# Coefficients placed three products sooner, a Gelu of one column ahead of each unit's Gelu, and the queries and keys in memory of their own

## The chip, the cores and the metric

The kernel runs on one core of one Trainium2 chip. The metric is the device time of one execution, in microseconds (us), with the median over several executions.

## What is computed

One inference step of two layers over 288 tokens: 256 tokens of a prompt and 8 sequences of 4 tokens each. Each layer has a token mixer (a gated convolution in the first layer, RWKV-7 in the second) and behind it a PEER channel mixer, which is the part that the change touches. Cut to that part:

```python
q = (hc @ wq).reshape(-1, PEER_HEADS, D_QUERY)
s1 = jnp.einsum('chd,hkd->chk', q[..., :half], k1)
s2 = jnp.einsum('chd,hkd->chk', q[..., half:], k2)
v1, i1 = lax.top_k(s1, PEER_TOPK)
v2, i2 = lax.top_k(s2, PEER_TOPK)
...
sc, ci = lax.top_k(cand, PEER_TOPK)      # the best 16 of 16 x 16 sums
eidx = e1 * N_KEYS + e2                  # 16 experts of 16384 per token and head
gate = jax.nn.softmax(sc, axis=-1)
z = jax.nn.gelu(jnp.einsum('cd,chkd->chk', hc, u_tab[eidx]), approximate=False)
coef = gate * z
return jnp.einsum('chk,chkd->cd', coef, v_tab[eidx])
```

Every token reads, for each of 8 heads, 16 rows of the table U and 16 rows of the table V, each row 1024 numbers in float32 (4 KB).

## The kernel before

**Units.** The 288 tokens times 8 heads make 2304 pairs, cut into 18 units of 128 pairs, one pair to a partition; the loop over them is `for lu in range(UNITS)` on every engine, and `u = u0 + lu` counts over both layers. A unit has 16 experts per pair, k = 0 to 15. For each k GpSimd issues one indirect transfer from U and one from V (`gather`, L1775), 128 rows of 4 KB each: 0.524 MB. So a unit is 32 transfers, 16.78 MB. U rows go to a ring of 8 slots, V rows to another ring of 8 slots, both in the buffer `ARENA`.

**Order on GpSimd.** Its queue is written by hand: in the steady part V(u, 0), U(u+1, 0), V(u, 1), U(u+1, 1), and so on (`experts` under `block.gpsimd`). It works in order. V(u, k) waits until the slot of product k-8 is free (`v_free`), U(u+1, k) until VectorE has used the slot of k-8 (`s_z`).

**VectorE** (`unit` in `experts` under `block.vector`) multiplies each landed U row with the token's row of h and sums it: `z_of(u + 1, k)`, L1380. Between these 16 products it does the small work of three units in order: it picks the experts of unit u+3 (`choose`, one piece behind each product from k = 3 on, the last piece, GX at L1331, behind product 15), spreads the indices of unit u+1 (`spread_indices`, L1359), turns them into V indices (`v_indices`, L1363), multiplies the Gelu of unit u with its gates (`spread_coefs`, L1368) and places the coefficients of unit u in the matrix ST (`place_coefs`, L1372).

**ScalarE** takes, for each unit, the Exp of GX for the softmax of unit u+3 (`gate_exp`, L1023) and the Gelu of the unit's 16 sums (L1058). Both need tables of their own, loaded by ACT_TABLE_LOAD.

**TensorE** regroups indices (`regroup_indices`, L580) and coefficients (`regroup_coefs`, L590) from pair to token order with four small products each, and then multiplies ST with the landed V rows: per unit four batches q = 0 to 3 of four k each, eight products a batch on four column groups at a time (L675). A batch frees its four V slots at its end, all at once:

```python
for q in range(TOPK // BATCH):
    for i in range(2):
        for j in range(BATCH):
            ...
            m = pe.matmul(ps[QUAD * j:QUAD * (j + 1), ACC_BANK + i, :], ST[:, k, :], ...)
    m.then_inc(v_free, BATCH)
```

**Start of a layer's experts.** The queries `Q4` and the keys `KT` lie in V slots 0 to 3, so the transfers V(0, 4) and later wait until the scores of all units are made, and the queue of GpSimd holds U(1, 0 to 11) ahead of them.

Of the kernel before, what the change touches and what calls it, by code (L numbers as in the profile page):

```python
# [8 lines left out]
ACT = mybir.ActivationFunctionType  # L9
# [139 lines left out]
def build(nc, a, out):  # L149
    with ExitStack() as ctx:  # L150
# [22 lines left out]

        N_RV, N_ROWS, N_SEL = 2 * RING * D, 3 * D, 2880
        ARENA = sb("ARENA", [N_RV + 2 * N_ROWS + N_SEL])
        RV = ARENA[:, 0:N_RV]
        OACC = ARENA[:, N_RV + N_ROWS:N_RV + 2 * N_ROWS].rearrange("p (a d) -> p a d", a=3)
        CURU = sb("CURU", [2, TOPK], U32)
# [33 lines left out]
        CS = carve(2 * DC * TOK + DC * UHW + DC * TOK, [DC * NS_TOK])  # L212
        Q4 = carve(RING * D, [4, TOK])
        KT = carve(RING * D + 1536, [2, HEADS, NKEYS])

        QP = carve(N_RV + N_ROWS, [16, P])
        HROW = ps[:, ROW_BANK:ROW_BANK + 2, :].rearrange("p b n -> p (b n)")


        sel0 = N_RV + 2 * N_ROWS  # L220
        SCUR = carve(sel0, [2, 2, NKEYS])
# [61 lines left out]
        OMKA = sb("OMKA", [DC])  # L283
        gst = sb("gst", [3, WHEADS])

        s_sh, s_shr = sem("shift_columns_ready"), sem("shift_rows_out")
# [41 lines left out]
        s_z = sem("z_done")  # L328
        s_gelu = sem("gelu_ready")
        s_im, s_ixp = sem("indices_spread"), sem("indices_regrouped")  # L330
        s_cm, s_cfp = sem("coefs_spread"), sem("coefs_regrouped")
# [154 lines left out]
        def _(pe):  # L486
# [85 lines left out]
            def regroup_indices(u):  # L572

                pe.wait_ge(s_im, u + 1)
                if u > 0:
                    pe.wait_ge(s_vidx, u)
                if u > 1:
                    pe.wait_ge(s_st, u - 1)
                for kk in range(4):
                    m = pe.matmul(ps[QUAD * kk:QUAD * (kk + 1), REGROUP_BANK, 0:TOPK], TURN[:, kk], IM.rearrange("p (q k) j -> p k q j", k=4)[:, kk],  # L580
                                  start=True, stop=True)
                m.then_inc(s_ixp, 1)

            def regroup_coefs(u):
                pe.wait_ge(s_cm, u + 1)
                if u > 0:
                    pe.wait_ge(s_st, u)
                pe.wait_ge(s_vidx, u + 2 if (u + 1) % UNITS else u + 1)
                for kk in range(4):
                    m = pe.matmul(ps[QUAD * kk:QUAD * (kk + 1), REGROUP_BANK, TOPK:2 * TOPK], TURN[:, kk], CM.rearrange("p (q k) j -> p k q j", k=4)[:, kk],  # L590
                                  start=True, stop=True)
                m.then_inc(s_cfp, 1)

            def experts(layer):
# [64 lines left out]
                for lu in range(UNITS):  # L659
                    u = u0 + lu  # L660
                    if lu in (7, 15):
                        rows_of_h((lu + 1) // 8)
                    if lu + 1 < UNITS:
                        regroup_indices(u + 1)
                    regroup_coefs(u)
# [3 lines left out]
# [3 lines that stand above are left out]
                                k = BATCH * q + j  # L672
                                if i == 0:
# [3 lines left out]
                                              stop=(lu in TILE_ENDS and q == 3), skip_group_check=True)  # L677
                        m.then_inc(v_free, BATCH)

                pe.wait_ge(acc_free, 2 * 3 * (layer + 1))  # L680
# [239 lines left out]
        def _(act):  # L920
# [85 lines left out]
            def experts(layer):  # L1006
# [48 lines left out]
                for lu in range(UNITS):  # L1055
                    u = u0 + lu
                    act.wait_ge(s_z, u * 16 + 16)
                    act.activation(GL[:, lu % 2, :], ZB[:, lu % 2, :], ACT.Gelu).then_inc(s_gelu, 1)  # L1058
# [107 lines left out]
        def _(v):  # L1166
# [183 lines left out]
            def experts(layer):  # L1350
# [56 lines left out]
                def unit(lu):  # L1407
# [7 lines left out]
                    else:  # L1415
                        chosen = choose(u + 3, layer) if lu + 3 < UNITS else iter(())
                    for k in range(TOPK):
                        if k == 2:
                            spread_coefs(u)
                            if 0 < lu and lu + 2 < UNITS:  # L1420
                                choose_ends(u + 2)
                        if k == 1:
                            spread_indices(u + 1)
                        if k == 3:
                            v_indices(u + 1)
                        if k == 5:
                            place_coefs(u)
                        z_of(u + 1, k)
# [290 lines left out]
        def _(pool):  # L1719
# [58 lines left out]
            def experts(layer):  # L1778
# [12 lines left out]
                def get_v(lu, k):  # L1791
                    u = u0 + lu
                    if k == 0:
                        pool.wait_ge(s_vidx, u + 1)
                    if lu == 0 and k == BATCH:

                        pool.wait_ge(bank_ready, GROUP[f"sc{layer}"] + 9)

                    pool.wait_ge(v_free, u * 16 + (k + 1))
                    gather(RVV, v_slot(k), v_tab, CURV[:, u % 2, k:k + 1], v_land)  # L1800

                for k in range(TOPK):
                    get_u(0, k)
                for k in range(BATCH):
                    get_v(0, k)
                for k in range(12):
                    get_u(1, k)
                for k in range(BATCH, TOPK):
                    get_v(0, k)
                    if k < 2 * BATCH:  # L1810
                        get_u(1, k + 8)
                for lu in range(1, UNITS):
# [73 lines left out]
```

## Time and profile before

| | |
|---|---|
| median of 3 runs | 2634.44 us (2632.85 to 2634.78) |
| the profiled execution | 2637.65 us, its span 2635.6 us |
| TensorE | 1690.9 us busy, 64% |
| VectorE | 1401.7 us busy, 53% |
| GpSimd | 1097.6 us busy, 42% |
| ScalarE | 307.3 us busy, 12% |
| queue of the indirect transfers | 604.05 MB, 59.5% of 16 DMA engines over the span |
| experts of the first layer | from 254 us to about 1100 us |
| RWKV layer's mixer | between about 1110 us and 1740 us, hardly any transfers |
| experts of the second layer | from 1783 us to about 2615 us |

Busy shares over the whole span mix stages with different limits. The columns to read here are those of a stretch: the share and the GB/s of the DMA engines, and beside an instruction the idle time of its engine before it and what ended that.

### The profile page before, as it was taken

Reading aid. Unit: us, or ns where it says so; the run is one execution under the profiler, and the core shown is the slowest. Engines: PE = TensorE matmul, PEld = TensorE weight load, DVE = VectorE, ACT = ScalarE, POOL = GpSimd, SP = SyncE. Lnnn points to the kernel's source line nnn. Section 1 sums busy time; section 2 is a strip of 40 time slices with the busy share of each in tenths; the row PEclk is TensorE's granted clock in tenths of the full one; section 3 lists DMA queues with packets and bytes.
Section 4 is the critical chain, followed back from the end, with each engine's and each line's share of the span. In section 5 each row is a group of like instructions: output and inputs, shape, how many; then the busy total and the mean of one; then the engine's idle time right before and its main releaser. Section 6 shows DMA issues by size and latency. Waiting matters only on the chain.

```text
span 2635.6 us, 23280 instructions
## 1 busy us (share of the span) xinstructions
PE 1690.9 (64%) x8416; PEld 877.0 (33%) x8416; DVE 1401.7 (53%) x3441; ACT 307.3 (12%) x589; POOL 1097.6 (42%) x1215
## 2 busy tenths in 40 slices
PE   6998754545354544699589897788545454444546
PEld 3776500000000010276389896466001010000102
DVE  1042766666666664322862634725766666666643
ACT  2211100000100000113221211012000001000000
POOL 2001566766666665300000000004666666666663
PEclk7999876667766676899789997699667666676668
DMA  8653899999999999724100002426999999999996
GB/s 358 282 205 123 337 357 371 381 372 374 383 359 385 366 387 384 264 109 159 57 1 1 1 1 106 160 79 241 366 390 357 387 366 386 362 389 365 384 365 249
DMA packets 177377, 722.65 MB, mean 274 GB/s; under 512 B 19824, under 2 KB 20336, under 8 KB 170480
## 3 DMA queue, kind: packets, MB, share of 16 engines
q0 software_dynamic: 165888, 604.05, 59.5%
q1 hardware_dynamic: 9216, 108.88, 10.5%
q10 hardware_dynamic: 2160, 8.24, 0.8%
q8 instruction: 67, 1.10, 0.2%
q14 instruction: 46, 0.38, 0.0%
HBM read 715.09 MB, written 6.01 MB: 274 GB/s over the span
## 4 chain that ended last, share of the span: by engine, by line
PE 36%; POOL 21%; DMA 18%; DVE 13%; issue 10%; ACT 1%; DVEq 0%; SPq 0%; POOLq 0%; ACTq 0%
POOL ARENA L1775 21%; PE ps L554 15%; DMA ARENA<-in_peer_u,CURU 14%; PE ps L675 6%; PE ps L790 5%; DVE ARENA L1380 3%; DMA ARENA<-in_peer_v,CURV 3%; DMA W<-in_w_ada 1%; PE ps L513 1%; PE ps L523 1%; DVE ST L1372 1%; PE ps L539 1%; PE ps L645 1%; DVE ARENA L1516 1%; PE ps L884 1%
## 5 line engine op out<-in xcount | busy, mean ns | idle before, releaser
L675 PE MATMUL ps<-ARENA,ST 128*32 128x512 f32 x2304 | 749.0, 881 | 563.7 <-DMA ARENA<-in_peer_v,CURV 364.7
L1775 POOL DMA_INDIRECT ARENA<-in_peer_u,CURU x576 | 540.7, 939 | 1141.3 <-DVE GX L1331 924.8
L1380 DVE SCALAR_TENSOR_TENSOR ARENA<-ARENA,ps 128x1024 f32<-128x1024 f32 x576 | 700.7, 1220 | 544.9 <-DMA ARENA<-in_peer_u,CURU 539.4
L1775 POOL DMA_INDIRECT ARENA<-in_peer_v,CURV x576 | 541.1, 939 | 364.0 <-PE ps L675 205.4
L675 PEld LDWEIGHTS ps<-ARENA,ST 128*32 128x32 f32 x2304 | 127.0, 140 | 1139.5 <-DMA ARENA<-in_peer_v,CURV 742.2
L554 PE MATMUL ps<-H,W 128*128 128x288 f32 x1024 | 261.0, 418 | 2.8 <-DVEq L1704 2.8
L554 PEld LDWEIGHTS ps<-H,W 128*128 128x128 f32 x1024 | 199.9, 196 | 58.9 <-DVEq L1704 3.0
L1023 ACT ACTIVATE GX<-GX 128x16 f32<-128x16 f32 x36 | 7.8, 216 | 1237.2 <-DVE GX L1331 1236.9
L790 PE MATMUL ps<-W 128*128 128x128 f32 (+1 forms) x1088 | 132.2, 285 | 20.6 <-DVEq L1176 20.4
L790 PEld LDWEIGHTS ps<-W 128*128 128x128 f32 (+1 forms) x1088 | 128.7, 199 | 24.1 <-DVEq L1176 23.1
L554 PE MATMUL ps<-ARENA,W 128*128 128x288 f32 x512 | 127.5, 413 | 0.0
L590 PE MATMUL ps<-ARENA,CONS 128*32 128x16 f32 x288 | 11.3, 220 | 163.7 <-DVE CURV L1363 163.7
L554 PEld LDWEIGHTS ps<-ARENA,W 128*128 128x128 f32 x512 | 99.0, 194 | 27.7
L1634 DVE TENSOR_TENSOR W<-W,ps 128x512 f32<-128x512 f32 (+1 forms) x76 | 50.6, 666 | 52.0 <-PE ps L790 51.1
L523 PE MATMUL ps<-W,CT 128*32 128x512 f32 x384 | 53.0, 686 | 31.5 <-DVEq L1176 13.1
L1226 DVE SCALAR_TENSOR_TENSOR X<-ps,ADA,X 128x256 f32<-128x256 f32 x32 | 15.5, 484 | 105.3 <-PE ps L554 52.2
L942 ACT ACTIVATE W<-ps 128x512 f32<-128x512 f32 (+2 forms) x81 | 46.5, 574 | 168.1 <-PE ps L790 147.4
L1194 DVE SCALAR_TENSOR_TENSOR GA<-ADA,PAR 128x72 f32<-128x72 f32 x4 | 0.9, 233 | 122.4 <-ACTq L1001 87.9
L1459 DVE SCALAR_TENSOR_TENSOR ARENA<-ARENA,PAR,H 128x288 f32<-128x288 f32 x48 | 21.8, 512 | 81.5 <-PE ps L554 80.5
L590 PEld LDWEIGHTS ps<-ARENA,CONS 128*32 128x32 f32 x288 | 8.4, 139 | 169.0 <-issue 166.1
L942 ACT ACTIVATE ARENA<-ps 128x288 f32<-128x288 f32 (+3 forms) x74 | 37.2, 516 | 182.4 <-PE ps L554 85.8
L580 PE MATMUL ps<-ARENA,CONS 128*32 128x16 f32 x288 | 9.8, 203 | 70.9 <-DVE ARENA L1359 70.9
(268 smaller groups left out, 1731.7 us busy)
## 6 DMA issues: line engine op xcount, KB each, us to landing
W<-in_w_ada SPq DMA_DIRECT2D x24, 2048.0 KB, 11.0
W<-in_peer_wq SPq DMA_DIRECT2D x8, 2048.0 KB, 8.1
W<-in_conv_w_in SPq DMA_DIRECT2D x6, 2048.0 KB, 14.1
ARENA<-in_peer_u,CURU POOLq DMA_INDIRECT x576, 6.9
ARENA<-in_peer_v,CURV POOLq DMA_INDIRECT x576, 6.9
W<-in_conv_w_out SPq DMA_DIRECT2D x2, 2048.0 KB, 9.9
W<-in_rwkv_wr SPq DMA_DIRECT2D x2, 2048.0 KB, 13.3
W<-in_rwkv_wk SPq DMA_DIRECT2D x2, 2048.0 KB, 9.5
```

What stands on the lines that cost most here:

```text
L513: m = pe.matmul(o[:, m4 * NCOND:(m4 + 1) * NCOND], ADR[j % 2][:, m4 * P:(m4 + 1) * P], sel[:, 0:NCOND], start=True, stop=True)
L523: m = pe.matmul(o[QUAD * g:QUAD * (g + 1), :], CT[:, k, 0:QUAD], W[:, t % WRING, k, :], start=(k < 4), stop=(k >= 4))
L539: m = pe.matmul(o[:, 0:TOK], ones[:], SQ[:, c, :], start=(c == 0), stop=(c == DC - 1))
L554: m = pe.matmul(o[:, 0:TOK], W[:, t % WRING, k, (m0 % 4) * P:(m0 % 4 + 1) * P], rhs[:, k, :], start=(k == 0), stop=(k == DC - 1))
L645: m = pe.matmul(o[:, j * P:(j + 1) * P], query_of(layer, 2 * h + half)[:, tile * P:(tile + 1) * P], KT[:, half, h, :], start=True, stop=True)
L675: m = pe.matmul(ps[QUAD * j:QUAD * (j + 1), ACC_BANK + i, :], ST[:, k, :], RVV[:, v_slot(k), i * 512:(i + 1) * 512], start=(lu % 8 == 0 an ...
L790: m = pe.matmul(o[0:n, j * n:(j + 1) * n], l[:, j, :], r[:, j, :], start=True, stop=True)
L884: pe.matmul(o, ART[:, c % 2, q].rearrange("p r t -> p (r t)"), SS[:, c % 2, q, :], start=(q == 0), stop=False, skip_group_check=True)
L942: act.activation(dst, src(o), func, **kw).then_inc(free, 1)
L1380: v.scalar_tensor_tensor(RU[:, k % RING, :], RU[:, k % RING, :], 1.0, HROW, ALU.mult, ALU.mult, accum_out=ZB[:, u % 2, k:k + 1]).then_inc( ...
L1634: V.do(v.tensor_tensor(dst, dst, o, ALU.add))
L1775: pool.indirect_dma_start(ring[:, slot, :], None, tab, bass.IndirectOffsetOnAxis(ap=idx, axis=0)).then_inc(landed[slot], 16)
```

## The change

It has four parts. On VectorE `spread_coefs(u)` moves from ahead of product 2 to ahead of product 1, `place_coefs(u)` from ahead of product 5 to ahead of product 2, `spread_indices(u + 1)` from product 1 to product 4 and `v_indices(u + 1)` from product 3 to product 8. On TensorE `regroup_indices(u + 1)` moves from ahead of unit u's coefficients to behind its second batch. On ScalarE a Gelu of one column stands ahead of the wait for the unit's sums. In `ARENA` the queries and keys get columns of their own, so GpSimd's queue at a layer's start issues V(0, 0 to 7), then U(1, 0 to 7), then V(0, k) and U(1, k) in turn.

```diff
-        N_RV, N_ROWS, N_SEL = 2 * RING * D, 3 * D, 2880
-        ARENA = sb("ARENA", [N_RV + 2 * N_ROWS + N_SEL])
+        N_RV, N_QK, N_ROWS, N_SEL = 2 * RING * D, 4 * TOK + 2048, 3 * D, 2752
+        ARENA = sb("ARENA", [N_RV + N_QK + N_ROWS + N_SEL])
...
-        Q4 = carve(RING * D, [4, TOK])
-        KT = carve(RING * D + 1536, [2, HEADS, NKEYS])
+        Q4 = carve(N_RV, [4, TOK])
+        KT = carve(N_RV + 4 * TOK, [2, HEADS, NKEYS])
...
                 if u > 0:
                     pe.wait_ge(s_vidx, u)
-                if u > 1:
-                    pe.wait_ge(s_st, u - 1)
+                    pe.wait_ge(s_st, u)
...
-                pe.wait_ge(s_vidx, u + 2 if (u + 1) % UNITS else u + 1)
+                pe.wait_ge(s_vidx, u + 1)
...
-                    if lu + 1 < UNITS:
-                        regroup_indices(u + 1)
                     regroup_coefs(u)
...
                         m.then_inc(v_free, BATCH)
+                        if q == 1 and lu + 1 < UNITS:
+                            regroup_indices(u + 1)
...
+                    if u > 0:
+                        act.wait_ge(s_warm, u)
+                    act.activation(warm[:], ident[:, 0:1], ACT.Gelu).then_inc(s_warm, 1)
                     act.wait_ge(s_z, u * 16 + 16)
...
                     for k in range(TOPK):
+                        if k == 1:
+                            spread_coefs(u)
                         if k == 2:
-                            spread_coefs(u)
+                            place_coefs(u)
                             if 0 < lu and lu + 2 < UNITS:
                                 choose_ends(u + 2)
-                        if k == 1:
+                        if k == 4:
                             spread_indices(u + 1)
-                        if k == 3:
+                        if k == 8:
                             v_indices(u + 1)
-                        if k == 5:
-                            place_coefs(u)
                         z_of(u + 1, k)
...
-                    if lu == 0 and k == BATCH:
-
-                        pool.wait_ge(bank_ready, GROUP[f"sc{layer}"] + 9)
-
...
-                for k in range(BATCH):
+                for k in range(RING):
                     get_v(0, k)
-                for k in range(12):
+                for k in range(RING):
                     get_u(1, k)
-                for k in range(BATCH, TOPK):
+                for k in range(RING, TOPK):
                     get_v(0, k)
-                    if k < 2 * BATCH:
-                        get_u(1, k + 8)
+                    get_u(1, k)
```

VectorE in unit 1 of the first layer, before, from the last small pieces behind product 15 on (L1380 is a product, L1359 `spread_indices`, L1368 `spread_coefs`, L1344 `choose_ends`, L1363 `v_indices`, L1372 `place_coefs`):

```order
L1380 SCALAR_TENSOR_TENSOR ARENA,ZB<-ARENA,ps 128x1024
L1359 TENSOR_TENSOR ARENA<-ARENA,CONS 128x64
L1380 SCALAR_TENSOR_TENSOR ARENA,ZB<-ARENA,ps 128x1024
L1368 TENSOR_TENSOR ARENA<-GL,ARENA 128x64
L1344 SCALAR_TENSOR_TENSOR ARENA<-GX,gsm,CONS 128x64
L1380 SCALAR_TENSOR_TENSOR ARENA,ZB<-ARENA,ps 128x1024
L1363 TENSOR_SCALAR CURV<-ps 128x16
L1380 SCALAR_TENSOR_TENSOR ARENA,ZB<-ARENA,ps 128x1024
...
L1380 SCALAR_TENSOR_TENSOR ARENA,ZB<-ARENA,ps 128x1024
L1290 MAX_INDEX ARENA<-ARENA,W 128x8
L1291 MATCH_REPLACE ARENA<-ARENA,W 128x128
L1372 TENSOR_TENSOR ST<-ps,CONS 128x512
```

The same place with the change (lines are four higher: L1384 is a product, L1372 `spread_coefs`, L1376 `place_coefs`, L1348 `choose_ends`, L1363 `spread_indices`):

```order
L1384 SCALAR_TENSOR_TENSOR ARENA,ZB<-ARENA,ps 128x1024
L1372 TENSOR_TENSOR ARENA<-GL,ARENA 128x64
L1384 SCALAR_TENSOR_TENSOR ARENA,ZB<-ARENA,ps 128x1024
L1376 TENSOR_TENSOR ST<-ps,CONS 128x512
L1348 SCALAR_TENSOR_TENSOR ARENA<-GX,gsm,CONS 128x64
L1384 SCALAR_TENSOR_TENSOR ARENA,ZB<-ARENA,ps 128x1024 x2
L1291 MAX ARENA<-W 128x8
L1292 MAX ARENA<-W 128x8
L1363 TENSOR_TENSOR ARENA<-ARENA,CONS 128x64
```

The placing of ST stood behind five products and two pieces of `choose` and now stands behind two products; the two steps for the next unit's indices moved behind it.

TensorE in the first two units, before (L580 is `regroup_indices`, L590 `regroup_coefs`, L675 the products with V):

```order
L655 MATMUL ps<-ARENA 128x128 x16
L580 MATMUL ps<-ARENA,CONS 32x16 x4
L590 MATMUL ps<-ARENA,CONS 32x16 x4
L675 MATMUL ps<-ARENA,ST 32x512 x32
L580 MATMUL ps<-ARENA,CONS 32x16 x4
```

The same place with the change (L581, L591 and L674 are the same three):

```order
L656 MATMUL ps<-ARENA 128x128 x16
L591 MATMUL ps<-ARENA,CONS 32x16 x4
L674 MATMUL ps<-ARENA,ST 32x512 x16
L581 MATMUL ps<-ARENA,CONS 32x16 x4
L674 MATMUL ps<-ARENA,ST 32x512 x16
```

The regrouping of the next unit's indices left the place ahead of the coefficients and splits the unit's 32 products in two halves.

GpSimd at the start of the first layer's experts, before:

```order
L1775 DMA ARENA<-in_peer_u,CURU 128x1024 x16
L1775 DMA ARENA<-in_peer_v,CURV 128x1024 x4
L1775 DMA ARENA<-in_peer_u,CURU 128x1024 x12
L1775 DMA ARENA<-in_peer_v,CURV 128x1024
L1775 DMA ARENA<-in_peer_u,CURU 128x1024
```

The same place with the change:

```order
L1779 DMA ARENA<-in_peer_u,CURU 128x1024 x16
L1779 DMA ARENA<-in_peer_v,CURV 128x1024 x8
L1779 DMA ARENA<-in_peer_u,CURU 128x1024 x8
L1779 DMA ARENA<-in_peer_v,CURV 128x1024
L1779 DMA ARENA<-in_peer_u,CURU 128x1024
```

Four V transfers moved ahead of unit 1's U transfers, and four U transfers moved behind the first V transfer that has to wait for TensorE.

## Rows read from the trace of the kernel before

**Rows 1.** Busy time by stretch: engines, TensorE clock, DMA share, GB/s.

```profile
core 0: us, PE busy (x) PEld busy (x) DVE busy (x) ACT busy (x) POOL busy (x), PEclk, DMA share, GB/s
...
950.35:1000.93 50.58, 21.38 (x148) 5.62 (x142) 24.58 (x61) 1.72 (x3) 29.98 (x32) 0.74 0.98 384
367.05:950.35 583.30, 281.18 (x1051) 52.55 (x1048) 370.93 (x963) 39.93 (x54) 390.76 (x416) 0.67 0.97 374
1891.64:2517.92 626.28, 301.02 (x1195) 58.02 (x1192) 398.88 (x1027) 41.65 (x57) 420.64 (x449) 0.68 0.97 376
1000.93:1046.20 45.27, 22.74 (x83) 4.06 (x82) 22.61 (x39) 1.30 (x3) 29.98 (x32) 0.68 1.02 405
...
1010.00:1045.00 35.00, 17.00 (x62) 3.16 (x65) 17.79 (x32) 1.30 (x3) 23.05 (x25) 0.60 1.03 410
```

**Rows 2.** GpSimd in order of time, unit 9 of the first layer, around its V(u, 8).

```profile
719.21 0.94 POOL L1775 DMA_INDIRECT ARENA<-in_peer_u,CURU  x1 [0.30 <-issue]
...
725.39 0.94 POOL L1775 DMA_INDIRECT ARENA<-in_peer_v,CURV  x1 [5.25 <-PE ps L675]
```

**Rows 3.** GpSimd's waits from 367 to 950 us: total, times, longest.

```profile
POOL ARENA L1775 <- issue: 116.8, 383, 0.3
POOL ARENA L1775 <- PE ps L675: 71.2, 20, 5.7
```

**Rows 4.** The stretch behind that wait, columns as in rows 1.

```profile
725.00:735.00 10.00, 5.73 (x24) 0.96 (x17) 4.98 (x14) 0.00 (x0) 7.48 (x8) 0.84 0.81 270
```

**Rows 5.** The same unit in order of time, ahead of that wait.

```profile
706.24 1.22 DVE L1380 SCALAR_TENSOR_TENSOR ARENA<-ARENA,ps 128x1024 f32<-128x1024 f32 x1 [0.45 <-DMA ARENA<-in_peer_u,CURU]
...
707.78 0.22 ACT L1023 ACTIVATE GX<-GX 128x16 f32<-128x16 f32 x1 [40.81 <-DVE GX L1331]
708.01 1.28 ACT L1058 ACT_TABLE_LOAD   x1
...
708.80 1.22 DVE L1380 SCALAR_TENSOR_TENSOR ARENA<-ARENA,ps 128x1024 f32<-128x1024 f32 x1 [0.40 <-DMA ARENA<-in_peer_u,CURU]
...
709.31 0.22 ACT L1058 ACTIVATE GL<-ZB 128x16 f32<-128x16 f32 x1
...
712.50 0.22 DVE L1368 TENSOR_TENSOR ARENA<-GL,ARENA 128x64 f32<-128x64 f32 x1
...
720.71 0.68 DVE L1372 TENSOR_TENSOR ST<-ps,CONS 128x512 f32<-128x512 f32 x1
...
721.45 6.86 PE L675 MATMUL ps<-ARENA,ST 128*32 128x512 f32 x32 [5.76 <-DVE ST L1372]
```

**Rows 6.** Transfers issued from 1010 to 1045 us: count, median us to landing.

```profile
ARENA<-in_peer_v,CURV POOLq DMA_INDIRECT x12, 8.1
```

**Rows 7.** Two batches' last products, once the fourth V row has landed.

```profile
345.42 1.90 PE L675 MATMUL ps<-ARENA,ST 128*32 128x512 f32 x10 [0.43 <-DMA ARENA<-in_peer_v,CURV]
...
391.13 3.62 PE L675 MATMUL ps<-ARENA,ST 128*32 128x512 f32 x10 [1.10 <-DMA ARENA<-in_peer_v,CURV]
```

**Rows 8.** SyncE's queue from 975 to 1100 us.

```profile
982.99 0.80 SPq L444 DMA_DIRECT2D W<-in_rwkv_wr  x2
```

**Rows 9.** Start of the first layer's experts and the first steady waits, in order of time.

```profile
278.97 1.00 POOL L1775 DMA_INDIRECT ARENA<-in_peer_v,CURV  x1 [0.30 <-issue]
291.12 0.94 POOL L1775 DMA_INDIRECT ARENA<-in_peer_u,CURU  x1 [11.14 <-DVE ARENA L1380]
...
309.36 0.23 DVE L1368 TENSOR_TENSOR ARENA<-GL,ARENA 128x64 f32<-128x64 f32 x1 [6.99 <-ACT GL L1058]
...
313.48 0.94 POOL L1775 DMA_INDIRECT ARENA<-in_peer_v,CURV  x1 [0.30 <-issue]
...
367.05 0.94 POOL L1775 DMA_INDIRECT ARENA<-in_peer_v,CURV  x1 [5.04 <-PE ps L675]
...
1845.13 0.94 POOL L1775 DMA_INDIRECT ARENA<-in_peer_v,CURV  x1 [0.31 <-issue]
...
1891.64 0.93 POOL L1775 DMA_INDIRECT ARENA<-in_peer_v,CURV  x1 [3.91 <-PE ps L675]
```

More of the change, by code:

```diff
@@ L171, in build @@
         W = sb("W", [WRING, DC, 512])
-        N_RV, N_ROWS, N_SEL = 2 * RING * D, 3 * D, 2880
-        ARENA = sb("ARENA", [N_RV + 2 * N_ROWS + N_SEL])
+        N_RV, N_QK, N_ROWS, N_SEL = 2 * RING * D, 4 * TOK + 2048, 3 * D, 2752
+        ARENA = sb("ARENA", [N_RV + N_QK + N_ROWS + N_SEL])
         RV = ARENA[:, 0:N_RV]
-        OACC = ARENA[:, N_RV + N_ROWS:N_RV + 2 * N_ROWS].rearrange("p (a d) -> p a d", a=3)
+        OACC = ARENA[:, N_RV + N_QK:N_RV + N_QK + N_ROWS].rearrange("p (a d) -> p a d", a=3)
         CURU = sb("CURU", [2, TOPK], U32)
@@ L212, in build @@
         CS = carve(2 * DC * TOK + DC * UHW + DC * TOK, [DC * NS_TOK])
-        Q4 = carve(RING * D, [4, TOK])
-        KT = carve(RING * D + 1536, [2, HEADS, NKEYS])
-        QP = carve(N_RV + N_ROWS, [16, P])
+        Q4 = carve(N_RV, [4, TOK])
+        KT = carve(N_RV + 4 * TOK, [2, HEADS, NKEYS])
+        QP = carve(N_RV + N_QK, [16, P])
         HROW = ps[:, ROW_BANK:ROW_BANK + 2, :].rearrange("p b n -> p (b n)")
-        sel0 = N_RV + 2 * N_ROWS
+        sel0 = N_RV + N_QK + N_ROWS
         SCUR = carve(sel0, [2, 2, NKEYS])
@@ L284, in build @@
         gst = sb("gst", [3, WHEADS])
+        warm = sb("warm", [1])
         s_sh, s_shr = sem("shift_columns_ready"), sem("shift_rows_out")
@@ L329, in build @@
         s_gelu = sem("gelu_ready")
+        s_warm = sem("gelu_table_loaded")
         s_im, s_ixp = sem("indices_spread"), sem("indices_regrouped")
```

## The prediction

> **What bounds the kernel now.** I read the busy time by stretch first. The two expert stages fill some 1600 us of the span, and in their steady parts no engine is full: from 367 to 950 us GpSimd is busy 390.8 of 583.3 us, VectorE 370.9, TensorE 281.2 [rows 1]. The DMA engines are: share 0.97 at 374 GB/s. These 583.3 us are 13 units (from V(u, 8) of unit 1 to that of unit 14), 44.87 us each; in the second layer 626.28 us are 14 units, 44.73 us each [rows 1].
>
> Is 374 GB/s the ceiling? No: from 1010 to 1045 us, with nothing held back, the same transfers run at 410 GB/s for 35 us [rows 1]. A unit is 16.78 MB (32 transfers of 0.524 MB), at 410 GB/s 40.9 us, or 1.28 us a transfer. So about 3.9 us of each unit are lost, and the order of time shows where. GpSimd issues U(u+1, 7) at 719.21 and V(u, 8) only at 725.39, idle for 5.25 us, released by TensorE's product with V [rows 2]. The waits give it 71.2 us in 20 times over the 13 units, nearly all in one long wait a unit; the usual gap is 116.8 / 383 = 0.30 us, so an issue takes 0.94 + 0.30 = 1.24 us [rows 2, 3]. Behind the wait the DMA engines starve: 270 GB/s for 10 us [rows 4], (410 - 270) x 10 = 1.4 MB or 3.4 us at 410, most of the 3.9.
>
> What does V(u, 8) wait for? Its slot is freed by batch q = 0 of unit u, which waits for ST, placed at 720.71; TensorE starts at 721.45 [rows 5] though its first rows have landed long ago: V(u, 3) is nine issues ahead of 719.21, at 708.0, and lands 7 to 8 us later. So the placing ends last, and it stands where it does only because VectorE works in order: the coefficients' Gelu was made at 709.31 [rows 5].
>
> **The placing, three products sooner.** Product 0 starts at 708.80 and takes 1.22 us; today `spread_coefs` starts behind product 1, at 712.50 [rows 5]. With the change it comes behind product 0, at about 710.1. The regrouping on TensorE has the whole of product 1 to end in (nothing is ahead of it any more but unit u-1's last batch, whose last V row was issued 2.5 us before V(u, 0)). The placing starts behind product 1, about 712.6, and takes 0.68 us [rows 5]: ST at 713.3 instead of 721.4, 8.1 us sooner. Now the rows end last: V(u, 3) is issued at 708.0. With 8.1 us to landing, what the saturated stretch shows [rows 6], it lands at 716.1. From the landing of a batch's fourth row to its end it takes 3.62 us or 1.90 us [rows 7], by TensorE's clock (0.60 to 0.74 is granted on the mean in these stretches [rows 1], between the levels of 1.2 and 2.4 GHz). So the slots come free at 719.7 or 718.0, and GpSimd wants them at 719.21 + 1.24 = 720.45. The wait is gone, with 0.7 us to spare at the slow clock.
>
> **What then sets the pace.** GpSimd can issue a unit in 32 x 1.24 = 39.8 us, the transfers need 41.0. So the DMA engines fall behind by 1.2 us a unit, landing times grow, and at about 8.8 us GpSimd begins to wait for V slots again, in pieces. Does that cost? With 8.8 us to landing at 1.28 us a transfer about seven transfers are under way; today 8.1 us goes with a full 410 GB/s [rows 1, 6]. A harder case is in the trace too: from 950.35 to 1000.93 two weight tiles (4.19 MB) are loaded beside the gathers [rows 8], GpSimd stands still, and the stretch still moves 384 GB/s with a share of 0.98 [rows 1]; a wait with a full queue costs nothing. I take 41.0 us a unit. Bounds: 39.8 (GpSimd's issue, if the DMA engines could follow) and 44.8 (nothing won).
>
> **Sum.** 13 units of 44.87 to 41.0: -50.3. 14 units of 44.73 to 41.0: -52.2. The unit with the weight tiles has 16.78 + 4.19 = 20.97 MB, 51.2 us at 410, and takes 50.58 today: +0.6. The units behind it in the first layer (45.27 us [rows 1]) and at the same place in the second: -4.3 and -3.7. The last unit of a layer starts from a deeper queue: +1 each, an estimate from 8.8 against 8.1 us, at two landings: +2.
>
> **Start of a layer.** Today V(0, 4 to 7) wait behind U(1, 11) in the queue. With the change they are issued from 280 us on, inside the 11.14 us in which GpSimd waits [rows 9] and the DMA engines run dry. The price: V(0, 8) now stands ahead of U(1, 8 to 11) and waits for batch 0. VectorE gets the Gelu at 309.36 [rows 9], the extra activation adds 0.2; product 1 and the placing add 1.9 (311.5), the batch 3.6: V(0, 8) at 315.2. From there 32 issues lead to V(1, 8), 39.8 us: 355.0, if U(2, 0), due at 337.6, finds its indices. It should: its selection goes two pieces a product from product 6 on and is complete behind product 12, near 334.5. The rest of unit 3's selection (some 6 us behind product 15, near 341) delays unit 1's Gelu to 349 and its batch 0 to about 355.5. So V(1, 8) comes at about 356 instead of 367.05 [rows 9]: -11, of which I take -10. In the second layer V(0, 4) is at 1845.13 against 313.48 in the first, an offset of 1531.65, so V(1, 8) comes at 1887.3 instead of 1891.64 [rows 9]: -4.3. Bounds for both together: -5 (if the held U transfers cost what the V transfers win) and -17.
>
> Sum: -50.3 - 52.2 + 0.6 - 8.0 + 2 - 14.3 = -122.2. The profiled execution takes 2637.65 us, so 2515.4; it lies 3.2 us above the median of 2634.44, so I expect **2512**.
>
> **The Gelu of one column** wins nothing, and I put it at 0. The table load stands at 708.01 because the Exp ahead of it, which needs another table, waits for GX, made behind product 15 (706.24 + 1.22); Exp, load and Gelu follow without a gap [rows 5]. The wait for the unit's sums is over by then, so a load "ahead" of it starts at the same moment, and the Gelu comes 0.22 us later, at 709.53 to 709.75, still before `spread_coefs` wants it at 710.1. If that cover is gone, VectorE waits some tenths, inside the 0.7 us above. In the first unit ScalarE is held by the scores' copies, likewise.
> The trace's load is 1.28 us, and from Exp to Gelu pass 1.53 us [rows 5]. The Trainium skill (ScalarE: Activation LUTs, "What ACT_TABLE_LOAD costs") counts a drain of 1.38 us to each switch, 2.66 us in all. By it the Gelu would come at 711.1 and VectorE would stand still for 1 us behind product 0; the trace shows no such drain, and even then nothing is added to the sum, for product 1 and the placing would still end ahead of V(u, 3)'s landing.
>
> **The indices, later.** `spread_indices` and `v_indices` move behind products 3 and 7. The new V indices are wanted at V(u+1, 0), eight pairs of issues (20 us) after V(u, 8), and product 7 ends some 8 us after V(u, 8): about 12 us of slack stay. Cost 0.
>
> **Rivals.**
> 1. *Part of the wait stays (0.12).* For it: 0.7 us to spare is thin at 1.2 GHz, and a batch frees four slots only at its end. Against it: the waits come with a full queue. If landing is uneven, so that single DMA engines idle, a unit takes 42.5 us: 29 units x 1.5 = 44 more, 2556.
> 2. *The DMA engines follow GpSimd (0.05).* 39.8 us a unit, 1.2 x 29 = 35 less: 2477. Against it: 410 GB/s never moves over 35 us while landing takes 8.1 us.
> 3. *The transfers are at their ceiling already (0.03).* Then the hole is made good elsewhere and only the start gains or nothing: 2620 to 2634. For it: the share is 0.97 today. Against it: the share counts a waiting engine as busy (0.81 at 270 GB/s [rows 4]), and 410 stands beside 374. The Trainium skill (DMA: Bandwidth & Descriptors, "Where 436 GB/s comes from") says the HBM side binds at about 358 GB/s per core for transfers from HBM; by that a unit would need 46.9 us and no order could help. This trace does not agree: 374 on the mean, 410 over 35 us.
> 4. *Slower (0.04): VectorE stalls at `v_indices`.* It now waits, ahead of product 8, for TensorE to end batch 1 of the unit before and regroup. V(u, 7) is issued 1.24 us ahead of U(u+1, 7), so the batch ends up to 3.62 us and the regrouping some 0.5 us after its landing, and VectorE comes to the place 1.28 + 1.22 us and a piece of `choose` (0.8) after it, 3.3: a wait of up to 0.8 us. Behind it stand product 8 and all later ones, and for them wait U slots. The ring of 8 gives 8 x 2.56 = 20.5 us for a landing (8.8), a product (1.2) and the wait: only above 10 us a unit does it hold GpSimd, and only above 14 does it take more than the 3.9 won. At 20 us it would be +6 us in each of 29 units, near 2800. Nothing in the trace makes TensorE so late, unless the two wait in a ring that I don't see.
>
> **How the numbers follow.** The forecast has 0.76; its own range is 2495 to 2535 (41.0 us a unit within 0.5, start within its bounds). With rivals 1 and 2 it makes faster 0.93. A change below 0.2%, 5 us, is about what a measurement of this kernel can't tell: same 0.03; slower 0.04. The range is 2480 to 2560: it leaves out rivals 2 to 4 and the upper half of rival 1, 0.18 in all.
>
> **What the new profile would show.** GpSimd's waits for TensorE of 5 us a unit gone, replaced by several below 1.5 us; units 41 us apart; 405 to 410 GB/s in each stretch of the steady part; landing 8 to 9.5 us; ST placed behind product 1; GpSimd's first wait of the layer at V(0, 8). I am wrong if TensorE's batch 0 ends later than 12 us after V(u, 3)'s issue in most units, or if GB/s stays below 395 without waits of GpSimd.

## The result and the profile after

The changed kernel takes **2521.82 us** (median of 4 runs, 2518.48 to 2523.70); the kernel before, run beside it, 2634.57 us (4 runs, 2632.85 to 2634.78). The ratio is 0.9572, with a 95% interval from 0.9555 to 0.9589: 113 us or 4.3% faster. The forecast was 2512, with a range of 2480 to 2560. The profiled execution takes 2523.46 us with a span of 2521.6; before it was 2637.65 with a span of 2635.6.

Busy time by stretch, changed kernel; it answers to [rows 1]. The first row covers 13 units of the first layer (V(1, 8) to V(14, 8)), the second the last ten of them, the third the unit behind, the fourth the unit with the weight tiles, the fifth 14 units of the second layer, the last 10 us picked for their low GB/s:

```profile
core 0: us, PE busy (x) PEld busy (x) DVE busy (x) ACT busy (x) POOL busy (x), PEclk, DMA share, GB/s
356.46:892.13 535.67, 325.85 (x1050) 53.93 (x1046) 368.33 (x962) 41.14 (x67) 392.18 (x417) 0.73 1.02 407
477.92:892.13 414.21, 246.39 (x809) 41.58 (x808) 284.16 (x740) 31.87 (x52) 302.04 (x321) 0.75 1.02 406
892.13:933.54 41.41, 25.06 (x142) 5.39 (x142) 28.09 (x72) 1.94 (x5) 30.15 (x33) 0.79 1.03 411
933.54:984.22 50.68, 24.07 (x82) 4.02 (x82) 20.63 (x36) 1.28 (x4) 29.97 (x33) 0.76 1.02 412
1826.69:2404.59 577.90, 354.39 (x1194) 59.87 (x1190) 396.77 (x1035) 43.07 (x72) 421.93 (x448) 0.74 1.02 407
...
710.00:720.00 10.00, 5.79 (x20) 0.90 (x20) 6.98 (x18) 3.09 (x5) 7.56 (x9) 0.66 0.98 370
```

13 units in 535.67 us are 41.21 us a unit, where they took 44.87; 14 in 577.90 are 41.28, where they took 44.73. The mean rate rose from 374 to 407 GB/s.

GpSimd's waits from 400 to 930 us, changed kernel (total, times, longest), to be held against [rows 3], and the median us to landing of the transfers issued in that stretch, to be held against [rows 6]:

```profile
POOL ARENA L1779 <- issue: 100.5, 323, 2.0
POOL ARENA L1779 <- PE ps L674: 21.7, 22, 2.3
POOL ARENA L1779 <- DVE ARENA L1384: 19.4, 60, 1.4
```

```profile
ARENA<-in_peer_u,CURU POOLq DMA_INDIRECT x206, 9.0
ARENA<-in_peer_v,CURV POOLq DMA_INDIRECT x205, 8.9
```

Over those same 530 us the kernel before waited 66.2 us for TensorE in 19 times, up to 5.7, and its transfers landed after 7.1 us. The 5 us wait is gone, and what is left comes in pieces of 1 us on the mean. GpSimd's waits for U slots (the row with L1384, the products on VectorE) have grown from 3.7 to 19.4 us: where the transfers set the pace, GpSimd is held back by both rings.

One unit of the changed kernel in order of time (unit 10 of the first layer), to be held against [rows 2, 5]; V(10, 3) is issued at 714.68, V(10, 8) at 727.15:

```profile
714.68 0.94 POOL L1779 DMA_INDIRECT ARENA<-in_peer_v,CURV  x1 [0.30 <-issue]
...
715.67 0.21 ACT L1024 ACTIVATE GX<-GX 128x16 f32<-128x16 f32 x1 [38.70 <-DVE GX L1335]
715.91 1.28 ACT L1060 ACT_TABLE_LOAD   x1
...
716.69 1.22 DVE L1384 SCALAR_TENSOR_TENSOR ARENA<-ARENA,ps 128x1024 f32<-128x1024 f32 x1 [0.40 <-DMA ARENA<-in_peer_u,CURU]
...
717.20 0.20 ACT L1060 ACTIVATE warm<-ident 128x1 f32<-128x1 f32 x1
717.31 0.20 ACT L1062 ACTIVATE GL<-ZB 128x16 f32<-128x16 f32 x1
...
719.23 1.22 DVE L1384 SCALAR_TENSOR_TENSOR ARENA<-ARENA,ps 128x1024 f32<-128x1024 f32 x1 [1.17 <-DMA ARENA<-in_peer_u,CURU]
...
720.37 0.69 DVE L1376 TENSOR_TENSOR ST<-ps,CONS 128x512 f32<-128x512 f32 x1
...
721.12 6.22 PE L674 MATMUL ps<-ARENA,ST 128*32 128x512 f32 x18 [2.75 <-DVE ST L1376]
721.12 0.19 PEld L674 LDWEIGHTS ps<-ARENA,ST 128*32 128x32 f32 x6 [2.85 <-DVE ST L1376]
...
723.03 0.20 PEld L674 LDWEIGHTS ps<-ARENA,ST 128*32 128x32 f32 x8 [1.72 <-DMA ARENA<-in_peer_v,CURV]
...
725.59 0.18 PEld L674 LDWEIGHTS ps<-ARENA,ST 128*32 128x32 f32 x2 [0.67 <-DMA ARENA<-in_peer_v,CURV]
...
727.15 0.94 POOL L1779 DMA_INDIRECT ARENA<-in_peer_v,CURV  x1 [0.30 <-issue]
```

Read it downward. Product 0 starts at 716.69; ST is ready at 721.06, 4.4 us later, where before it was 12.6 us later (708.80 and 721.39 in [rows 5]). Batch 0 starts as soon as ST is there: a product has two weight loads here, so the six at 721.12 are those of the rows k = 0 to 2. The fourth row, V(10, 3), is taken at 723.03, when it has landed, 8.35 us after its issue. (The load at 725.59 is the first of batch 1 and waited for V(10, 4).) V(10, 8), 12.47 us after V(10, 3), goes out with the usual 0.30 us. The table load stands behind the Exp as before: `L1060`'s load is the one that stood at Gelu's line, moved by nothing.

The 40 slices of the page show the same at a glance: 401 to 412 GB/s through both expert stages, but for their ends.

```profile
GB/s 374 256 246 100 312 406 409 409 409 409 403 403 409 401 412 409 205 109 167 34 1 1 1 1 79 126 155 205 312 409 410 409 408 404 407 402 408 409 403 230
```

### The profile page after: what moved, and what is told of

Its sections match the earlier page's. It is cut to its first block, busy times and chain, and to the rows that moved or that the text cites. A ratio compares the mean times of both kernels' runs of the same rounds, so it can differ in the third digit from the quotient of the medians.

```text
span 2521.6 us, 23313 instructions
## 1 busy us (share of the span) xinstructions
PE 1781.4 (71%) x8416; PEld 875.9 (35%) x8416; DVE 1398.7 (55%) x3441; ACT 310.4 (12%) x625; POOL 1100.6 (44%) x1215
## 4 chain that ended last, share of the span: by engine, by line
PE 35%; DMA 29%; POOL 15%; DVE 11%; issue 7%; ACT 2%; DVEq 0%; SPq 0%; POOLq 0%; ACTq 0%
DMA ARENA<-in_peer_u,CURU 17%; PE ps L556 15%; POOL ARENA L1779 15%; DMA ARENA<-in_peer_v,CURV 11%; PE ps L791 5%; PE ps L674 4%; DVE ARENA L1384 3%; DMA W<-in_w_ada 1%; PE ps L515 1%; PE ps L525 1%; PE ps L541 1%; PE ps L646 1%; DVE ARENA L1520 1%; DVE W L1630 1%; PE ps L867 1%
## 5 line engine op out<-in xcount | busy, mean ns | idle before, releaser
L674 PE MATMUL ps<-ARENA,ST 128*32 128x512 f32 x2304 | 854.2, 893 | 501.3 <-DMA ARENA<-in_peer_v,CURV 411.8
L1384 DVE SCALAR_TENSOR_TENSOR ARENA<-ARENA,ps 128x1024 f32<-128x1024 f32 x576 | 700.0, 1220 | 421.5 <-DMA ARENA<-in_peer_u,CURU 416.8
L674 PEld LDWEIGHTS ps<-ARENA,ST 128*32 128x32 f32 x2304 | 130.7, 134 | 1146.0 <-DMA ARENA<-in_peer_v,CURV 882.5
L1230 DVE SCALAR_TENSOR_TENSOR X<-ps,ADA,X 128x256 f32<-128x256 f32 x32 | 15.5, 483 | 103.9 <-PE ps L556 51.8
L591 PE MATMUL ps<-ARENA,CONS 128*32 128x16 f32 x288 | 9.6, 199 | 81.7 <-DVE ARENA L1372 81.7
L1463 DVE SCALAR_TENSOR_TENSOR ARENA<-ARENA,PAR,H 128x288 f32<-128x288 f32 x48 | 21.7, 512 | 81.1 <-PE ps L556 80.2
L591 PEld LDWEIGHTS ps<-ARENA,CONS 128*32 128x32 f32 x288 | 6.0, 114 | 127.1 <-DVE ARENA L1372 127.1
L515 PE MATMUL ps<-sel,scr 128*128 128x9 f32 x120 | 21.5, 308 | 37.7 <-ACT scr L943 37.7
```

Source lines behind the costliest of these rows:

```text
L515: m = pe.matmul(o[:, m4 * NCOND:(m4 + 1) * NCOND], ADR[j % 2][:, m4 * P:(m4 + 1) * P], sel[:, 0:NCOND], start=True, stop=True)
L1384: v.scalar_tensor_tensor(RU[:, k % RING, :], RU[:, k % RING, :], 1.0, HROW, ALU.mult, ALU.mult, accum_out=ZB[:, u % 2, k:k + 1]).then_inc( ...
```

## Experiments

Eight kernels, each timed against the kernel before in the same session. start_only, place_only, no_warm and release_two shared one session (before: 2633.22), early_first and the three place_k kernels another (before: 2634.20). Unit times are the distances from V(u, 8) to V(u+1, 8) in GpSimd's timeline, the time of a layer's start is the distance from its first U transfer to V(1, 8). All are from one profiled execution each; the first U transfer itself stands between 249.3 and 254.4 us in them, so distances are compared, not places.

**1. The new start alone (start_only).** The kernel before, with only the arena and GpSimd's start order of the change:

```diff
-        N_RV, N_ROWS, N_SEL = 2 * RING * D, 3 * D, 2880
+        N_RV, N_QK, N_ROWS, N_SEL = 2 * RING * D, 4 * TOK + 2048, 3 * D, 2752
...
-                for k in range(BATCH):
+                for k in range(RING):
                     get_v(0, k)
-                for k in range(12):
+                for k in range(RING):
                     get_u(1, k)
```

> Queries and keys in columns of their own and the new order of GpSimd's queue at a layer's start, with all else as before. My theory: only the two starts gain, 14 us by my sum less what the old place of the coefficients takes back, so 2620 to 2630 us, and the units stay 44.8 us apart with one wait of 5 us each. Rival, the start carries much of the gain: below 2600 us.

Measured: 2633.46 us (10 runs, 2628.39 to 2634.89), ratio 0.9998 (0.9988 to 1.0008). Nothing, where I had expected 2620 to 2630. V(0, 8) stands at 317.27 and has waited 16.94 us; the layers' starts take 109.8 and 110.2 us (before 112.7 and 108.6). V(0, 8) itself comes sooner after the first U transfer (65.0 and 65.1 us, before 69.1 and 72.0), but the way from there to V(1, 8) is longer (44.7 and 45.1 us, before 43.6 and 36.6). My reading: the placing is still late, so V(0, 8) waits for it, and with it the U transfers that now stand behind it. Experiments 6 to 8 bear on this: with the new start kept and the placing moved back, the starts grow with every product.

**2. The new places alone (place_only).** The changed kernel with the old arena and the old start order, and without the activation of one column:

```diff
-                for k in range(RING):
+                for k in range(BATCH):
                     get_v(0, k)
-                for k in range(RING):
+                for k in range(12):
                     get_u(1, k)
...
-                    if u > 0:
-                        act.wait_ge(s_warm, u)
-                    act.activation(warm[:], ident[:, 0:1], ACT.Gelu).then_inc(s_warm, 1)
```

> The new places of coefficients and indices alone, with the start of a layer and the memory as before and without the Gelu of one column. My theory (the placing released V slots too late and starved the DMA engines): units 41.3 us apart as with the whole change, GpSimd's 5 us waits gone, and about 100 of the 113 us: 2532 to 2540 us. Rival, the start carries much of the gain: above 2560 us.

Measured: 2539.50 us (4 runs, 2535.28 to 2542.05), ratio 0.9640 (0.9622 to 0.9658). The units take 41.10 and 41.15 us, as in the changed kernel: the steady gain is here in full. But the starts now take 115.1 and 113.4 us, more than before. Busy time from 320 to 330 us, then VectorE in order of time, and GpSimd's waits behind it:

```profile
320.00:330.00 10.00, 5.18 (x6) 0.54 (x6) 0.00 (x0) 0.00 (x0) 6.31 (x7) 0.50 1.03 412
```

```profile
333.94 0.18 DVE L1364 TENSOR_SCALAR CURV<-ps 128x16 uint32<-128x16 f32 x1 [15.50 <-PE ps L581]
```

```profile
334.09 0.94 POOL L1776 DMA_INDIRECT ARENA<-in_peer_v,CURV  x1 [5.95 <-PE ps L674]
340.99 0.99 POOL L1776 DMA_INDIRECT ARENA<-in_peer_v,CURV  x1 [2.24 <-DVE ARENA L1381]
345.88 0.93 POOL L1776 DMA_INDIRECT ARENA<-in_peer_u,CURU  x1 [3.91 <-DVE GX L1332]
```

This is the mechanism of rival 4, once a layer: VectorE (the third number pair of the first row, 0.00) does nothing for 15.5 us ahead of product 8 (12.5 us in the second layer), since the regrouping of the indices now stands behind batch 1, and batch 1's rows V(0, 4 to 7) stand behind U(1, 11) in the old start order. GpSimd then waits 12.1 us in three places.

**3. The stall taken away (early_first).** place_only, but in the first unit of each layer the indices are spread, regrouped and taken early (the regrouping, on TensorE, ahead of the coefficients; that part of the edit is left out here):

```diff
                         if k == 1:
+                            if lu == 0:
+                                spread_indices(u + 1)
                             spread_coefs(u)
...
...
-                        if k == 8:
+                        if k == (8 if lu else 3):
                             v_indices(u + 1)
```

> The kernel with the new places alone (measured at 2539.5 us, its layer starts 9 us longer than with the whole change), but in the first unit of each layer the next unit's indices are spread, regrouped and taken as early as in the kernel before. My theory: that kernel loses its 18 us because VectorE waits ahead of product 8 for TensorE's second batch, which waits for V rows issued late in the old order. So the wait goes, V(1, 8) comes 8 to 12 us earlier after the layer's first U, and the time is 2518 to 2528 us. Rival, the loss is the V transfers themselves, which the new order moves into idle DMA time: 2535 to 2542 us, no change.

Measured: 2529.93 us (4 runs, 2526.80 to 2530.40), ratio 0.9603 (0.9588 to 0.9618), 9.6 us below place_only and 8.1 us above the changed kernel. The starts take 110.0 and 104.9 us (changed kernel: 102.1 and 103.1), and the stall of 15.5 us is gone. So of the 17.7 us that the new start is worth on top of the new places, some 10 are this stall, which the new start takes away by issuing V(0, 4 to 7) first; the other 8 or so are the start order itself. The split is rough, since place_only ran in the other session: measured from each session's kernel before, it is 10.6 and 7.1. I had expected 2518 to 2528: a narrow miss.

**4. Without the activation of one column (no_warm).**

```diff
-                    if u > 0:
-                        act.wait_ge(s_warm, u)
-                    act.activation(warm[:], ident[:, 0:1], ACT.Gelu).then_inc(s_warm, 1)
```

> The whole change without the Gelu of one column. My theory: it wins nothing, the same time within 0.1% of the changed kernel (2519 to 2525 us), since the Exp ahead of it ends after the sums are there. Rival, the table load was on the path of the coefficients: each unit 0.3 to 1.3 us longer, 2530 us or more.

Measured: 2521.85 us (5 runs, 2520.75 to 2524.46), ratio 0.9583 (0.9569 to 0.9598): the changed kernel's time, within what such a measurement can tell. The edit is worth nothing, and costs nothing.

**5. V slots freed two at a time (release_two).** The changed kernel; TensorE takes each batch's rows in two pairs and frees two slots behind each:

```diff
-                        for i in range(2):
-                            for j in range(BATCH):
+                        for two in range(2):
+                            for i in range(2):
+                                for j in (2 * two, 2 * two + 1):
...
-                        m.then_inc(v_free, BATCH)
+                            m.then_inc(v_free, 2)
```

> The whole change, and TensorE takes the V rows two at a time and frees two slots at a time instead of four. Theory A, what is left of the loss (41.3 to 41.5 us a unit where 410 GB/s would give 40.9) are GpSimd's waits for slots that come free four at a time: those waits vanish, landing grows beyond 9 us, units 41.0, 2510 to 2515 us. Theory B, the rest is in the DMA engines' own rate, which dips for a few us now and then with GpSimd never late: waits vanish, the time stays at 2519 to 2525 us. Theory C, the DMA engines can follow GpSimd's 39.8 us a unit when never held back: 2485 us or less.

Measured: 2517.48 us (5 runs, 2514.17 to 2518.62), ratio 0.9559 (0.9544 to 0.9574), 4.4 us below no_warm in the same session, and the ranges don't meet. It is the fastest kernel of this study. It falls between the two theories that I had given, 2510 to 2515 us and 2519 to 2525 us, and both had the waits vanish. GB/s in 40 slices from 400 to 930 us, the landing times, and GpSimd's waits there:

```profile
GB/s 410 408 409 409 409 410 409 410 409 409 409 408 409 409 410 410 409 410 409 409 409 409 409 409 410 410 409 408 410 409 407 403 410 409 379 412 411 410 407 411
...
ARENA<-in_peer_u,CURU POOLq DMA_INDIRECT x207, 12.1
ARENA<-in_peer_v,CURV POOLq DMA_INDIRECT x206, 12.1
```

```profile
POOL ARENA L1780 <- PE ps L675: 20.4, 17, 2.5
```

Landing grows to 12.1 us, three microseconds more queue than the change has, and yet the rate is 408 for 407 on the mean, still 409 to 410 in most slices, and GpSimd waits 20.4 us for TensorE, with the change 21.7. The V(u, 8) of the first layer stand at 356.0, 395.8, 435.5, 475.4, 517.4 us: three units at 39.8 us, GpSimd's own pace, and one of 41.9; from there to V(14, 8) at 890.4 the units average 41.4. So the settled pace is not GpSimd's. The four units from V(1, 8) to V(5, 8) take 1.9 us less than with the change in the first layer and as much less in the second, which is the filling of the deeper queue; what is left of the 4.4 us, and what the higher clock of TensorE in this kernel (at the end of this text) has to do with them, is not shown.

**6 to 8. The placing moved back step by step (place_k3, place_k4, place_k5).** The changed kernel, with `place_coefs(u)` ahead of product 3, 4 or 5; `spread_coefs`, the indices and the start stay new:

```diff
                         if k == 2:
-                            place_coefs(u)
                             if 0 < lu and lu + 2 < UNITS:
                                 choose_ends(u + 2)
+                        if k == 4:
+                            place_coefs(u)
```

> The whole change with the coefficients placed ahead of product 3 instead of 2. My theory: V(u, 3)'s landing and the placing then end within 1 us of each other, the pace is still the DMA engines', landing settles near 8.2 us instead of 9.0, 2519 to 2526 us. Rival, every 2.6 us of later placing are paid: unit 0.8 us or more longer, 2545 us or more.

> The same ahead of product 4. My theory: the slots come free only if landing takes under about 6 us, where the DMA engines just fill; units of 41.5 to 42.5 us, 2527 to 2555 us, and landing near 6 to 7 us. Rival, paid in full: 2580 us or more.

> The same ahead of product 5, where the kernel before has it, with the indices at their new places and the new start of a layer. My theory: the wait of 4 to 5 us a unit is back and with it the hole behind it, units of 44 to 45 us, 2605 to 2630 us. Rival, the moved indices or the regrouping's new place on TensorE gave part of the gain: below 2590 us.

Measured:

| placed ahead of product | us, median (runs, range) | ratio (95%) | unit, layers 1 and 2 | starts, layers 1 and 2 | landing, us (V) |
|---|---|---|---|---|---|
| 2 (the change) | 2521.82 (4, 2518.48 to 2523.70) | 0.9572 (0.9555 to 0.9589) | 41.20, 41.26 | 102.1, 103.1 | 8.9 |
| 3 | 2525.06 (5, 2524.21 to 2527.49) | 0.9590 (0.9577 to 0.9603) | 41.22, 41.23 | 105.8, 106.4 | 8.7 |
| 4 | 2546.86 (4, 2545.20 to 2554.17) | 0.9681 (0.9665 to 0.9697) | 42.07, 42.03 | 107.1, 108.4 | 6.8 |
| 5 (place of before) | 2639.72 (9, 2636.31 to 2640.98) | 1.0017 (1.0007 to 1.0027) | 44.84, 45.04 | 111.9, 111.6 | 6.6 |

The unit times here are over the 13 units from V(1, 8) to V(14, 8) of each layer.

Busy time by stretch and then GpSimd's waits, both from 400 to 930 us, first of the kernel with 4, then of the kernel with 5:

```profile
400.00:930.00 530.00, 271.73 (x1022) 49.91 (x1018) 358.72 (x934) 38.05 (x62) 382.08 (x406) 0.74 1.02 399
```

```profile
POOL ARENA L1780 <- PE ps L674: 36.6, 29, 3.7
```

```profile
400.00:930.00 530.00, 246.20 (x968) 50.58 (x968) 336.31 (x878) 38.04 (x62) 355.51 (x378) 0.69 0.97 374
```

```profile
POOL ARENA L1780 <- PE ps L674: 66.2, 22, 6.5
```

The kernel with 5 has every other part of the change and none of its gain; its profile is that of before, down to the 374 GB/s and the 66.2 us of waits. And its placing is late though `spread_coefs` is early. Its VectorE around V(u, 8) of one unit, then GpSimd:

```profile
703.24 0.22 DVE L1372 TENSOR_TENSOR ARENA<-GL,ARENA 128x64 f32<-128x64 f32 x1
...
714.00 0.68 DVE L1376 TENSOR_TENSOR ST<-ps,CONS 128x512 f32<-128x512 f32 x1
```

```profile
718.68 0.94 POOL L1780 DMA_INDIRECT ARENA<-in_peer_v,CURV  x1 [4.87 <-PE ps L674]
```

The wait of 4.87 us ends 4.7 us after the placing has started. The gain is not linear in the place. From 5 to 4 a unit of the first layer wins 2.8 us (two products stand 2.54 us apart in the unit shown above), from 4 to 3 only 0.85, from 3 to 2 nothing: the pace has met another limit by then. The starts do go on gaining from 3 to 2, 7.0 us in both layers together. I had expected 2605 to 2630 of the last kernel, some gain being left to the start; it came out 5.5 us above before (its profiled execution 2.9). Its starts take 2.2 us more than before's, so the new start wins nothing where the placing is late, as in start_only; its second-layer units take 0.3 us more each (4 us), and why, I did not test.

## Why the prediction was right

**What bounds the kernel.** Right. The DMA engines were not at their ceiling at 374 GB/s; 410 GB/s, read from 35 us behind the last steady unit, was it. 407 GB/s on the mean over 530 us is what remains with dips in it.

The Trainium skill has a rule that made rival 3 (DMA: Bandwidth & Descriptors, "Where 436 GB/s comes from": about 358 GB/s per core on the HBM side). By it the change could have won nothing; the runs, with 407, do not agree with it. The page gets the figure by dividing the 716 GB/s of a stack by two cores, and this kernel runs on one.

**The placing as the thing that ends last.** Right, and shown by place_k5: undoing this one move gives the whole 113 us back. Also right that the rows end last once it is moved: in the unit shown above batch 0 has started at 721.12 when its fourth row comes, at 723.03. The placing has 1.9 us to spare there, and nearly the same in most units of the layer; by the forecast's own figures it had 2.8 (ST at 713.3, the row at 716.1). The forecast let product 1 end by the clock of before, but product 1 waits for its own U row (the 1.17 us at 719.23), so it moves with the transfers.

The 0.7 us of the forecast was another one, between the release of the slots and GpSimd's need. It was not needed to the full: in place_k3 the placing comes some 2.5 us later, GpSimd waits 0.7 to 2.0 us at V(u, 8) in each unit from 4 to 14 of the first layer, and a unit still takes 41.22 us. Its waits from 400 to 930 us:

```profile
POOL ARENA L1780 <- PE ps L674: 25.6, 25, 2.0
```

place_k5 shows that the move of the placing is needed, not that it suffices. In the kernel before, TensorE could not regroup the coefficients before the indices of the next unit had been taken:

```profile
715.38 0.31 PE L590 MATMUL ps<-ARENA,CONS 128*32 128x16 f32 x8 [4.85 <-DVE CURV L1363]
```

Without the later indices the placing could not have come at 713. Their move is a part of the gain's cause; no kernel has the early placing with the indices left in their old places throughout.

**The pace that follows.** The mechanism right, the size off. I took 41.0 us a unit from 16.78 MB at 410 GB/s; measured are 41.2 and 41.3, in the settled ten units 41.42. Rates of 408 to 412 GB/s do hold in 34 of the 40 slices of 13.25 us below, but six fall to 376 to 407, as from 710 to 720 us above (370). Against 410 the six lack 112 GB/s together, which over 13.25 us is 1.48 MB, 3.6 us, or 0.28 us in each of the 13 units. I had read the ceiling from 35 us that held no such dip.

GB/s in 40 slices from 400 to 930 us, changed kernel:

```profile
GB/s 411 409 410 408 409 410 408 409 409 410 410 409 409 409 409 410 409 400 388 410 410 409 407 376 412 410 410 408 410 408 409 410 389 388 411 410 409 409 409 409
```

What makes the dips is open. They fall behind the places where GpSimd waited longest or twice in a short time (1.41 and 1.64 us at 622.9 and 634.3, 1.62 and 0.96 us at 696.5 and 707.2, 2.27 us at 831.7), though 1.76 us at 499.6 and 1.80 at 903.5 have no dip behind them. In release_two, with landing at 12.1 us, more than nine transfers of 1.28 us are outstanding, and its waits of 2.1 to 2.5 us pass without a dip but for one (379); its four slices below 408 lack 44 GB/s together in place of 112. So a shallow queue behind a wait may make a part of the dips. It isn't shown: no_warm lacks 110 and place_only 68 with the same landing as the change, and a wait can as well follow from rows that landed late. Rival 1 (part of the wait stays, 42.5 us a unit) did not come in this kernel, but it is what place_k4 shows: with the placing two products later the waits are 36.6 us, the rate is 399 GB/s and a unit takes 42.07. Rivals 2 and 3 did not come.

**The unit with the weight tiles and the one behind it.** Right: 41.41 + 50.68 us in place of 50.58 + 45.27, -3.8 against the -3.7 forecast (-3.7 from 892.09, where V(14, 8) itself stands). The tiles' 10 us moved by one unit. In the second layer the unit at that place won 2.8 against 3.7. **The last units:** +0.9 and +0.8 (from V(16, 8) to the last V transfer), forecast +1 each.

**The starts.** V(1, 8) stands at 356.46 (forecast 356), 10.6 us sooner than before for a forecast 10, and the second layer's start is 5.5 us shorter (forecast 4.3). GpSimd at both places:

```profile
315.43 0.93 POOL L1779 DMA_INDIRECT ARENA<-in_peer_v,CURV  x1 [14.62 <-PE ps L674]
...
356.46 0.94 POOL L1779 DMA_INDIRECT ARENA<-in_peer_v,CURV  x1 [1.33 <-PE ps L674]
```

The wait at V(0, 8) is where it was forecast, at 315.4 for 315.2. The 14.3 us hold for the new start together with the early placing, from which I had worked them out, though the sum has them as a term of its own. They can't be had apart: alone the new start wins 0 (start_only), on top of the new places 17.7 (2539.50 to 2521.85), more than the forecast's 14.3 since the new places alone make the starts longer (115.1 and 113.4 us for 112.7 and 108.6), which I had not seen. The two parts are one change: the moved regrouping of the indices needs V(0, 4 to 7) early (early_first), and the early V rows need the early placing (start_only and place_k5).

**Indices later, cost 0.** Right in the steady part: VectorE's waits there are 6.6 us in ten times from 400 to 930 us, at most 0.7, where I allowed 0.8. At the start of a layer it is 0 only because of the new start order (place_only: 15.5 us).

```profile
DVE CURV L1367 <- PE ps L581: 6.6, 10, 0.7
```

**The activation of one column.** Right, 0 (no_warm). The load ahead of it starts when the load ahead of Gelu did, behind the Exp, and Gelu follows. From the Exp (715.67) to the activation behind the load (717.20) pass 1.53 us, so the drain of 1.38 us that the Trainium skill counts to a switch (ScalarE: Activation LUTs, "What ACT_TABLE_LOAD costs") is not in this trace either.

**The sum.** Of the 114.0 us by which the spans of the profiled executions differ (2635.6 and 2521.6), the 13 units give 47.7 (forecast 50.3), the 14 units 48.4 (52.2), the weight tiles' pair 3.7 (3.7), the unit after the 14 units 2.8 (3.7), the starts 16.1 (14.3), the last units -1.7 (-2); what lies between the layers and behind the last V transfer took 3.0 us more (0). The forecast, 122.2, was 8.2 us too large in all: 7.3 of it is the unit's size, 41.0 for 41.2 to 41.3; the 3.0 us between and behind the stages, which I had not costed, is mostly made up by the starts' extra 1.8 and the last units' 0.3, and that is luck. To the median I had gone down by 3.2 us, the distance that the profiled execution of before had; the one of after lies 1.6 above its median, and that is the other part of 2521.8 against 2512.

**The signs.** Not all that the new profile was to show came. The waits for TensorE reach 2.3 us for the 1.5 named, the rate falls below 405 GB/s in stretches of 10 us (370), and batch 0 ends about 12 us after V(u, 3)'s issue (8.35 to the landing in the unit above, and 3.62 to the end by [rows 7]), just where I had set the bound of being wrong. It did no harm, since V(u, 8) is wanted only 12.4 us after V(u, 3).

## What to carry to other kernels

Where one queue issues for two consumers in turn, look at what releases the slot that it waits for, and then at what stood last ahead of that release; here it was a short step on VectorE that waited for nothing but its place in the program order, and moving it, with the steps that stood in its way, was worth 3.6% by itself (place_only) and 4.3% with the new start, with no work removed. Move such a step until the next thing ends last and no further: two of the three products' worth of move brought nearly all (2639.7, 2546.9, 2525.1, 2521.8). Take the new ceiling from as long a stretch as there is, with its dips, and test two parts that share a buffer or an order together and apart: 0 alone can be 18 together.

## What the runs showed of the hardware

- Gathers of 0.524 MB (128 rows of 4 KB) from HBM run at 408 to 412 GB/s for most of 530 us on one core, with single stretches of 10 to 13 us at 370 to 400 whose cause is not known; there are five slices of 13 us at 400 or less with landing at 9 us and one at 12 us.
- The depth of the queue shows in the time to landing: at 6.8 us to landing and waits of up to 3.7 us the rate is 399 GB/s (place_k4), at 8.7 us 407 (place_k3), at 12.1 us 408 (release_two). The rate hardly grows beyond some seven transfers outstanding, an estimate from 8.9 us at 1.28 us each. Depth and waits change together in these kernels, so their effects are not apart.
- TensorE's granted clock is higher in the faster kernels: from 400 to 930 us it is 0.67 before, 0.74 with the change and 0.86 in release_two, where TensorE takes its rows two by two (busy 256.1, 321.6 and 314.3 us, the clocks are means between the levels of 1.2 and 2.4 GHz). What raised it, and whether any of release_two's 4.4 us come from it, I did not test.

```profile
400.00:930.00 530.00, 314.32 (x1094) 65.12 (x1096) 363.62 (x944) 39.98 (x67) 389.12 (x413) 0.86 1.03 408
```
